# Prompt attention with two buffers of biased scores, scores issued two tiles ahead and outputs taken two tiles late

## The reference

```python
def diff_attn_prompt(qa, ka, va, lam):
    def block(args):
        qi, i = args
        d = (i * Q_BLOCK + jnp.arange(Q_BLOCK))[:, None] - kpos[None, :]
        w = diff_weights(diff_scores(qi, k, d.astype(jnp.float32), d >= 0), lam)
        return jnp.einsum('bhqk,bkhe->bqhe', w.astype(va.dtype), va)
...
def diff_weights(s, lam):
    p = jax.nn.softmax(s, axis=-1)
    return p[:, 0] - lam * p[:, 1]
```

## Time and profile before

| What | us |
|---|---|
| Median of 3 runs | 4031.53 |
| Profiled execution, its own time | 4029.83 |
| Its span, first to last instruction | 4028.3 |
| Mixer A of the prompt, first matmul to last output | 386.5 to 556.2 |
| Wait for the loads of mixer B | 558 to 592 |
| Mixer B of the prompt, first matmul to last output | 594.2 to 768.0 |
| DVE idle in mixer A, waiting for `exps` | 34.5 |
| DVE idle in mixer A, waiting for PE before `output` | 22.3 |

### The profile page before, as it was taken

The page is one execution under the profiler, slowest core; times in us unless marked ns, Lnnn a source line. Parts: engine busy times, 40 slices in busy tenths (PEclk is TensorE's granted clock), DMA queues, the critical chain, the costliest instruction groups (busy, mean ns, idle before and its releaser), DMA issues. The chain is left out here.

```text
span 4028.3 us, 63885 instructions
## 1 busy us (share of the span) xinstructions
PE 3241.9 (80%) x22587; PEld 2883.4 (72%) x22587; DVE 2865.9 (71%) x6550; ACT 1213.7 (30%) x2349; POOL 1214.1 (30%) x1219
## 2 busy tenths in 40 slices
PE   7997749777772763565461999999999999999998
PEld 5875537555552661333241999999999999999998
DVE  6462634279999961111116999999999999999998
ACT  5452425322223980121111222222222222222221
POOL 0000000000000001444111456555566556555554
PEclk9998979988886995787675999999999999999999
DMA  3322142133331999999733999999999999999997
GB/s 137 113 73 89 55 154 65 46 126 110 122 113 61 307 316 298 387 387 343 298 135 144 333 341 330 339 346 350 347 332 339 349 350 340 333 344 345 341 336 283
DMA packets 408387, 1002.69 MB, mean 249 GB/s; under 512 B 38371, under 2 KB 166469, under 8 KB 406789
## 3 DMA queue, kind: packets, MB, share of 16 engines
q0 software_dynamic: 150048, 595.57, 40.5%
q1 hardware_dynamic: 253716, 386.23, 27.5%
q10 hardware_dynamic: 4448, 18.87, 1.2%
HBM read 921.60 MB, written 146.44 MB: 265 GB/s over the span
## 5 line engine op out<-in xcount | busy, mean ns | idle before, releaser
L1832 PE MATMUL banks<-x_hi,u_hi 128*128 128x320 f32 x2048 | 634.2, 310 | 86.7 <-DVE x_lo L1922 86.7
L1845 PE MATMUL banks<-coef_hi,v_hi 128*128 128x320 f32 x2048 | 633.9, 310 | 6.1 <-issue 6.1
L1832 PE MATMUL banks<-x_lo,u_hi 128*128 128x320 f32 x2048 | 633.9, 310 | 0.0
L1832 PE MATMUL banks<-x_hi,u_lo 128*128 128x320 f32 x2048 | 633.9, 310 | 0.0
L1845 PE MATMUL banks<-coef_lo,v_hi 128*128 128x320 f32 x2048 | 633.7, 309 | 0.0
L1845 PE MATMUL banks<-coef_hi,v_lo 128*128 128x320 f32 x2048 | 633.6, 309 | 0.0
L1793 POOL DMA_INDIRECT uv_row<-in_v_rows,expert_tok x384 | 477.9, 1245 | 386.3 <-DVE y_tok L1976 334.6
L1793 POOL DMA_INDIRECT uv_row<-in_u_rows,expert_tok x384 | 456.2, 1188 | 362.6 <-DVE dots L1950 315.2
L1976 DVE SCALAR_TENSOR_TENSOR y_tok<-uv_row,share,y_tok 128x1024 f32<-128x1024 f32 x415 | 530.7, 1279 | 0.7
L1950 DVE CUSTOM_DVE_ANT_0 uv_row<-uv_row,x_tok 128x1024 f32<-128x1024 f32 x416 | 506.7, 1220 | 0.0
L1832 PEld LDWEIGHTS banks<-x_hi,u_hi 128*128 128x128 f32 x2048 | 385.5, 188 | 87.1 <-DVE x_lo L1922 87.1
(11 more groups left out here) (265 smaller groups left out, 5611.8 us busy)
## 6 DMA issues: line engine op xcount, KB each, us to landing
keys_sa<-in_cache_k SPq DMA_DIRECT2D x256, 256.0 KB
values_sa<-in_cache_v POOLq DMA_DIRECT2D x256, 256.0 KB, 6.7
uv_raw<-in_u SPq DMA_DIRECT2D x128, 512.0 KB
uv_raw<-in_v SPq DMA_DIRECT2D x128, 512.0 KB
scratch_gates<-stage SPq DMA_DIRECT2D x10, 4096.0 KB, 29.5
gates<-scratch_gates SPq DMA_DIRECT2D x128, 320.0 KB
out_win_k_out<-in_state_k POOLq DMA_DIRECT2D x8, 4088.0 KB
out_win_v_out<-in_state_v POOLq DMA_DIRECT2D x8, 4088.0 KB
```

What stands on the lines that cost most here:

```text
L1832: ins = nc.tensor.matmul(bank[:, 2 * r + c, 0:CH], u[r][a][:, k * P:(k + 1) * P], x2[b][:, k, c * CH:(c + 1) * CH], start=(k == 0 and a == b),
L1845: ins = nc.tensor.matmul(bank[:, 4 + n % 4, 0:CH], v[j][a][:, k * P:(k + 1) * P], coef[j][b][:, c * CH:(c + 1) * CH], start=(j == 0 and a ...
```

## The change

`neg_scores` gets a second buffer, and the loops of PE, DVE and ACT are reordered. Line numbers behind the second hunk grow by one or two. The rest of the program is as before.

```diff
-        neg_s = sb("neg_scores", [P, 2, SEQ])
+        neg_s = sb("neg_scores", [P, 2, 2, SEQ])
...
                 scores(turn, 0)
+                scores(turn, 1)
                 for n in range(TURN_TILES):
-                    if n + 1 == QT:
+                    transpose_weights(turn, n)
+                    if n + 2 == QT:
                         pe.wait_ge(loaded[1], turn * 80 + 80)
-                    if n + 1 < TURN_TILES:
-                        scores(turn, n + 1)
-                    transpose_weights(turn, n)
+                    if n + 2 < TURN_TILES:
+                        scores(turn, n + 2)
                     if n:
                         weigh_values(turn, n - 1)
                 weigh_values(turn, TURN_TILES - 1)
...
-                    since(dve, exp_done, turn * (2 * TURN_TILES) + max(0, 2 * n + m - 1))
+                    since(dve, exp_done, turn * (2 * TURN_TILES) + max(0, 2 * n + m - 3))
                     nc.vector.memset(gate[:, 2 * n + m:2 * n + m + 1], 0.0)
                     nc.vector.tensor_tensor_reduce(
-                        neg_s[:, m, 0:L], bank[:, 2 * m:2 * m + 2, :].rearrange("p b c -> p (b c)")[:, 0:L],
+                        neg_s[:, n % 2, m, 0:L], bank[:, 2 * m:2 * m + 2, :].rearrange("p b c -> p (b c)")[:, 0:L],
...
                 for n in range(TURN_TILES):
-                    combine(turn, n)
                     if n + 1 == QT:
                         dve.wait_ge(loaded[1], turn * 80 + 80)
                     if n + 1 < TURN_TILES:
                         bias(turn, n + 1)
-                    if n:
-                        output(turn, n - 1)
+                    combine(turn, n)
+                    if n > 1:
+                        output(turn, n - 2)
+                output(turn, TURN_TILES - 2)
                 output(turn, TURN_TILES - 1)
...
-                    nc.scalar.activation(e[:, n % 2, m, 0:L], neg_s[:, m, 0:L], ACT.Exp, bias=neg_max[:, n % 2, m:m + 1],
+                    nc.scalar.activation(e[:, n % 2, m, 0:L], neg_s[:, n % 2, m, 0:L], ACT.Exp, bias=neg_max[:, n % 2, m:m + 1],
...
                 for n in range(TURN_TILES):
-                    take_weights_T(turn, n)
                     if n + 1 < TURN_TILES:
                         exps(turn, n + 1)
+                    take_weights_T(turn, n)
```

## The result

| | before | changed |
|---|---|---|
| median, us | 4031.53 | 4049.66 |
| lowest to highest, 5 runs | 4027.40 to 4032.56 | 4047.53 to 4054.41 |
| profiled execution, us | 4029.83 | 4050.43 |
| mixer A, first matmul to the barrier behind its last store | 171.7 | 190.0 |
| mixer B, the same | 175.9 | 175.0 |

The changed kernel is slower: 1.0047 times the time before, 95% interval 1.0033 to 1.0062. The forecast was 4055, between 4038 and 4070. Of the 20.6 us between the two profiled spans, mixer A has 18.3 and mixer B -0.9. The last 3.2 lie outside both: 4.5 more behind mixer B, 1.2 less ahead of the mixers and between them. No line was changed behind mixer B, and that stretch took between 3254.8 and 3264.0 us in the kernels of this case, without a pattern.

The account below looks back on a forecast made before the run. Mixer A was taken as bound by DVE's work plus pauses, mixer B by PE's. Pauses 7, cold start 2, clock 13 and mixer B 1 gave 23 us more: 4055 us, range 4038 to 4070.

Parts of the forecast that it names:

- wait for exponentials: Mixer A: all 28 waits of DVE for ACT's exponentials go, 34.5 us saved.
- pauses of a unit at full clock: Mixer A: DVE's new pauses ahead of the first and second bias, 11.9 us a unit, 47.7 for four.
- change of unit: Mixer A: DVE's pauses where one unit follows another, 1.2 + 1.5 us, twice: 5.4.
- start of a turn: Mixer A: DVE waits for tile 1's scores, and two passes have no output as cover: 3.0 us for both turns.
- end of a turn: Mixer A: DVE waits while PE transposes and does two tiles of values, about 4.0 us, 8.0 for both turns.
- cold start: Mixer A, first turn at half clock: transposes and scores now stand on the path at the start, 2 us.
- falls of the clock: Mixer A: PE's longer pauses lower its clock in half of 24 pauses, 1.1 us each: 13 us, between 0 and 41.
- mixer B: Mixer B: ACT's copies come late behind the next tile's exponentials, 0.3 to 0.4 us in four units: 1 us.
- The formula for DVE's pause: Mixer A: pause ahead of bias(n + 2) is 0.15 + 0.117 k + 0.22 b us, 0.93 to 2.61 for k = 1 to 6.
- The rival that went with it, 4042: Mixer A: PE's clock holds, so only 10 us are left: 4042 us; chance 0.22.
- the rival at 4065: Mixer B: ACT's copies hold up PE, 11 us: 4065 us; chance 0.05.
- The faster rival: Mixer A: scores(n + 2) are ready when DVE reaches the bias, no new pauses: 3989 us; chance 0.06.

Follow-up runs that it names:

- experiment 5: Changed kernel plus twelve idle transposes (the fillers) on PE behind the values in mixer A, only at tiles 1 to 6 of a unit: 4039.59 us.
- Experiment 1: Changed kernel with PE's scores of tile n + 2 moved ahead of the transposes of tile n: 3985.85 us, 0.9879 of the kernel before.
- experiment 6: The changed kernel again with no edit, timed beside the kernel with idle transposes: 4051.67 us, 1.0050 of the kernel before.
- experiments 2 and 3: 2: changed kernel with PE's order of before, 4133.87 us; 3: the same with ACT's order of before in mixer B alone, 4095.36 us.
- experiments 4 and 5: 4: changed kernel plus twelve idle transposes on PE in each pass of mixer A, 4041.65 us; 5: only behind tiles 1 to 6, 4039.59 us.

## Why the prediction was right

The mechanism was the forecast's; the sizes, term by term:

| step | forecast, us | measured, us | where |
|---|---|---|---|
| wait for exponentials | -34.5 | -34.5 | no row of it left |
| pauses of a unit at full clock, 4 times | 11.9 | 11.55 | second unit of experiment 5 |
| change of unit, twice | 1.2 + 1.5 | 1.19 + 1.43 | first change of the changed kernel |
| start of a turn, twice | 1.5 | 0.58 + 0.37 + 0.26 = 1.21 | second turn, the last two against its second unit |
| end of a turn, twice | 4.0 | 2.55 + 1.49 = 4.04 | second turn, full clock |
| cold start | 2 | 2.4 | first turn against the second |
| falls of the clock | 12 x 1.1 = 13 | 8, together 10.6 | pause by pause, see below |
| mixer A | +22 | +18.3 | |
| mixer B | +1 | -0.9 | |
| the rest | 0 | +3.2 | |

With the 22.3 us of waits ahead of outputs that were there before, the measured terms of mixer A add up to 18.1.

**The wait that was added.** The formula for DVE's pause was built from rows of a kernel that had no such pause, and its 1.60, 1.94, 2.28 and 2.61 us for 5 to 8 blocks were measured as 1.53, 1.85, 2.17 and 2.50 where the clock held: 0.1 too long. For 3 and 4 blocks, 0.93 and 1.26 were 0.71 and 1.14. The waits for the second map were 0.05 too short (0.44 at 8 blocks, 0.49 measured) or a little more, so the sum for a unit is 0.35 too high. Without its falls mixer A is 18.3 - 10.6 = 7.7 us longer than before, and the terms without a fall gave 7 + 2 = 9. One term has no working that leads to it: at the end of a turn, 4.35 + 1.50 us less the 0.8 that 8 transposes gain at full clock is 5.05 and not "about 4.0", and that 4.04 was measured is luck. Experiment 1 settles the reason of the pauses: transposes ahead of the scores, on an engine that took its matmuls in the order of the program here.

**The falls.** This is the term that was mis-sized most, in both factors. Half of 24 pauses were to bring one, at 1.1 us each. There were eight. At five of the six that DVE waits for, its pauses are 1.61 to 1.69 us longer than the same pauses at full clock, at the sixth (496.0) 1.19; the one at the end of the first turn (475.5) cost 1.39 + 2.17 + 1.49 - 4.04 = 1.0, and the eighth next to nothing. That is 10.6 us, and fewer falls at a higher price came near 13 by luck. The fillers give back 7.9 in the profiled stage; the other 2.9 are their late cold start and the fall that they leave. The 2.4 us too many are most of the 3.7 by which mixer A came out shorter than forecast. That no fall would come at the change of unit was right for the scores; one lay on the values there (at 523.3), and DVE's pause behind it was 1.47 instead of 1.43 us. In experiment 6 there was one at each of the two changes, and the first held up scores too (1.64 us instead of 1.19).

The number of falls was taken from two pauses in another phase, because "no row shows such a pause in this stage". The trace of the kernel before does show some of the shorter ones: PE paused 1.0 to 1.5 us ahead of the transposes of small tiles, and its clock fell behind none of these pauses. The longest:

```profile
442.36 0.66 PE L577 MATMUL banks<-ident,weights_a 128*128 128x128 f32 x4 [1.48 <-DVE weights_a L643]
```

By the section of the Trainium skill that the forecast weighed (TensorE: Matmul & The Clock Gate, HAM oscillation) a fall comes from a single longer gap. PE's longest pause in mixer A behind the cold start was 2.46 us, and the clock fell there all the same: the measurement decides against the rule, as the rows behind mixer B had suggested. The rival that went with it, 4042, is near what experiment 5 makes of the kernel by holding the clock: 8.9 us over the kernel before, timed beside it, where that rival said 10.

**Mixer B** moved by -0.9 us. The waits for ACT's copies rose by 0.8, not by the whole pauses that the rival at 4065 needed; experiments 2 and 3 show that this rival's mechanism is real and needs scores that come late.

**The faster rival,** 3989 us if the scores start before the combine ends, was priced well: experiment 1 fulfils its condition and took 3985.85, which is 47.0 less than the kernel before, timed beside it, where that rival said 42.5.

Left open: the 3.2 us outside the mixers have no cause in any trace here.

## What to carry to other kernels

A distance in the program is a distance on the engine only if nothing that waits stands ahead: work that is made in advance goes in front of the instruction that waits for the other engine, in every engine's order. Here three edits were one schedule: scores ahead of the transposes, exponentials ahead of the copies and outputs two tiles late are worth 47 us together (3985.85 against 4032.82 of the kernel before, timed beside it), and with any one of them left out (the outputs with one buffer only) the kernel was no faster than before, while the second buffer was not needed. When two engines wait for each other in turn, add the price of PE's clock to the price of the pauses, and try filling the gaps to see which of the two is paid.

## What the runs showed of the hardware

The length of one pause of PE does not tell whether the clock falls: in the first unit it fell after 2.13 us and held after 2.24 and 2.35 (the transposes at 406.75, 414.60 and 421.61 above). In another execution of the same program the falls lay in part at other tiles, and one came behind a pause of 2.25 us at the tile that had kept its clock. In all, eight or nine of some 25 pauses of 1.5 to 2.5 us brought one, 18 of 30 when the longest were 3.6 us (experiment 2), and with idle transposes in the pauses only one was left, at the start of the second turn (experiments 4 and 5). A fall lasted 3.4 us in the changed kernel. It cost DVE 1.2 to 1.7 us where it waited for slowed scores, 1.0 at the end of a turn, and 0.04 where the slowed matmuls were nearly covered.
